# Mixer C's upward products as twelve pairs by Strassen's algorithm; the last two blocks' downward products joined there and in the first feed-forward layer

## What is computed

```
h = rmsnorm(x);  y = concat(a_out, b_out) @ w_out           # stage 0, mixer A/B
h = rmsnorm(x);  z = h @ w_up; g, up = split(z)             # stage 1, feed-forward layer 1, D_FF = 2816
                 y = (silu(conv3(g)) * up) @ w_down
h = rmsnorm(x);  z = h @ w_in; bg, cg, hx = split(z)        # stage 2, mixer C, width 1024
                 y = (bg * conv3(cg * hx)) @ w_out
h = rmsnorm(x);  ...                                        # stage 3, feed-forward layer 2
y = rmsnorm(x, norm_final)
```

## Time and profile before

| | us |
|---|---|
| median of 3 runs | 2181.38 (2180.86 to 2185.6) |
| the profiled execution | 2185.06, its span 2183.2 |
| PE busy | 2130.8 (98% of the span) |
| DVE, ACT, POOL busy | 1444.9 (66%), 675.8 (31%), 884.2 (40%) |
| from the last pair of stage 1 to the first matmul of stage 3 | 423.00 |

### The profile page before, as it was taken

The page is one execution under the profiler, slowest core; times in us unless marked ns, Lnnn a source line. Parts: engine busy times, 40 slices in busy tenths (PEclk is TensorE's granted clock), DMA queues, the critical chain, the costliest instruction groups (busy, mean ns, idle before and its releaser), DMA issues. The chain is left out here.

```text
span 2183.2 us, 35348 instructions
## 1 busy us (share of the span) xinstructions
PE 2130.8 (98%) x15116; PEld 2118.0 (97%) x15116; DVE 1444.9 (66%) x1765; ACT 675.8 (31%) x1002; POOL 884.2 (40%) x540
## 2 busy tenths in 40 slices
PE   6999999999999999999999999999999999999996
PEld 6999999999999999999999999999999999999996
DVE  5899769766666666666653524497666666766666
ACT  4555245322223322222311011263222223322233
POOL 4766234444434443434412221344343444444345
PEclk9999999999999999999999999999999999999998
DMA  4111210111111111111111111101111111111112
GB/s 160 39 39 41 109 61 30 59 39 59 39 59 59 49 40 49 59 40 59 49 39 49 49 49 39 49 30 45 53 57 41 59 59 40 39 59 49 49 42 80
DMA packets 33996, 115.31 MB, mean 53 GB/s; under 512 B 3824, under 2 KB 7408, under 8 KB 33840
## 3 DMA queue, kind: packets, MB, share of 16 engines
q1 hardware_dynamic: 33840, 113.06, 15.0%
HBM read 108.42 MB, written 4.62 MB: 52 GB/s over the span
## 5 line engine op out<-in xcount | busy, mean ns | idle before, releaser
L606 PE MATMUL psum<-xs_hi,w_hi 128*128 128x264 f32 (+1 forms) x3728 | 1112.7, 298 | 32.7 <-DVE xs_lo L1609 17.2
L608 PE MATMUL psum<-xs_hi,w_lo 128*128 128x264 f32 (+1 forms) x3728 | 1110.3, 298 | 0.0
L607 PE MATMUL psum<-xs_lo,w_hi 128*128 128x264 f32 (+1 forms) x3728 | 1106.3, 297 | 0.0
L1044 POOL TENSOR_TENSOR w_lo<-raw,w_hi 128x512 fp32r<-128x512 f32 (+1 forms) x358 | 595.0, 1674 | 983.5 <-ACT w_hi L1221 624.2
L606 PEld LDWEIGHTS psum<-xs_hi,w_hi 128*128 128x128 f32 x3728 | 702.6, 188 | 39.1 <-issue 11.4
L608 PEld LDWEIGHTS psum<-xs_hi,w_lo 128*128 128x128 f32 x3728 | 703.3, 189 | 0.0
L607 PEld LDWEIGHTS psum<-xs_lo,w_hi 128*128 128x128 f32 x3728 | 702.6, 188 | 0.0
L606 PE MATMUL psum<-act_hi,w_hi 128*128 128x352 f32 x1152 | 373.3, 324 | 0.1
L608 PE MATMUL psum<-act_hi,w_lo 128*128 128x352 f32 x1152 | 373.1, 324 | 0.0
L607 PE MATMUL psum<-act_lo,w_hi 128*128 128x352 f32 x1152 | 370.5, 322 | 0.0
L1620 DVE TENSOR_TENSOR x<-psum,x 128x704 f32<-128x704 f32 x208 | 185.0, 889 | 163.0 <-PE psum L608 162.2
(11 more groups left out here) (233 smaller groups left out, 1757.3 us busy)
## 6 DMA issues: line engine op xcount, KB each, us to landing
raw<-slabs SPq DMA_DIRECT2D x188, 512.0 KB, 3.2
x<-x_t SPq DMA_DIRECT2D x16, 528.0 KB, 6.9
y_t<-x SPq DMA_DIRECT2D x6, 528.0 KB, 3.4
y_t<-x SPq DMA_DIRECT2D x3, 352.0 KB, 2.3
x<-mix SPq DMA_DIRECT2D x1, 512.0 KB, 3.3
x<-bs SPq DMA_DIRECT2D x1, 256.0 KB, 3.9
tail_hi<-consts SPq DMA_DIRECT2D x1, 132.0 KB, 11.2
const<-consts SPq DMA_DIRECT2D x1, 130.0 KB, 4.4
```

What stands on the lines that cost most here:

```text
L606: nc.tensor.matmul(out, w_hi[:, w], hi, start=start, stop=False, skip_group_check=reopen)
L607: nc.tensor.matmul(out, w_hi[:, w], lo, start=False, stop=False, skip_group_check=reopen)
L608: return nc.tensor.matmul(out, w_lo[:, w], hi, start=False, stop=stop, skip_group_check=reopen)
L1044: nc.gpsimd.tensor_tensor(w_lo[:, slab], src, w_hi[:, slab].bitcast(F32), ALU.subtract).then_inc(weights_ready, 1)
```

## The change

1. **Mixer C in pairs.** The 24 upward tiles become twelve pairs in the code of the feed-forward stages: for each of four blocks of two channel tiles, (Cg, hx) of the first, (Cg, hx) of the second, and (Bg of the first, Bg of the second). `_units` lists three pairs a block for stage 2, `down` for blocks 0 and 1, and a `join` at the end. All three pairs use one up buffer, `prod[0]`; PSUM sets alternate by `x_set`.
2. **Joins.** The last two blocks' downward products of stages 1 and 2 are one pass over four activation tiles (`join`), eight output tiles of 4 products x 3 chunks x 3 = 36 matmuls, so that the next stage's normalised input is made as each output tile ends (`last_down`). Stage 1 had two passes of two before.
3. **Start.** 44 transposes of the identity on PE ahead of the data; ACT makes all eight high parts before any square; DVE makes all the sums of squares; ACT copies the first tile out of PSUM unscaled; the statistics stand after five of eight input tiles of the second job and the spread after all of them.
4. **Mixer A/B.** One GpSimd tap of channel tile 2 moves from slot 8 to slot 9 of `A_PLAN`.
5. **End.** The last product's chunks are 400, 400 and 256 frames; DVE makes all outputs of the second and third chunk; the second chunk's spread stands after the last matmul.

The diff, cut to its core: `up_free` is ACT's, ahead of its copy of group 0's result into the up buffer, `c_gate` (Cg x hx), `finish` and the second `join` are DVE's (the tables for semaphore counts, renamings and the host's packing of weights are left out):

```diff
+WARM_UP = 44
-FINAL_ROWS = [[(CUTS[c] + 88 * t, 88) for t in range(4)] for c in range(3)]
+FINAL_CUTS = (0, 400, 800, COLS)
+FINAL_ROWS = [[(FINAL_CUTS[c] + rows * t, rows) for t in range(n)] for c, (n, rows) in enumerate([(4, 100), (4, 100),
+                                                                                                (2, P)])]
+def _units(p):
+    pairs, last = (3 if p == 2 else 2), BLOCKS[p] - 1
+    units = []
+    for b in range(last + 1):
+        units += [("pair", b, q) for q in range(pairs)]
+        if b and (b < last or p == 3):
+            units.append(("down", b - 1))
+    return units + [("down", last) if p == 3 else ("join", last)]
...
+            def first_jobs():
+                up_job(0, 0, 0, fresh=True)
+                ring1 = slab_ready(1)
+                up_part(1, ring1, range(0, 5))
+                pe.wait_ge(tile_evacuated, evacuated(0))
+                pe.wait_ge(squares_summed, DVE_SUMS)
+                rms_stats(0, psum[:, 0, CH + 2:CH + 2 + ROW_TILES])
+                up_part(1, ring1, range(5, KD)).then_inc(tile_done, 1)
+                rms_spread(0, psum[:, 3, CH + 30:CH + 30 + ROW_REST])
...
+            for _ in range(WARM_UP):
+                nc.tensor.transpose(psum[:, 7, 0:P], ident[:], ident[:])
...
+            def join(p, unit):
+                acts = ACT0[p] + 2 * unit[1] - 2
+                for m in range(KD):
+                    if m % 2 == 0:
+                        pe.wait_ge(weights_ready, step_of(p, unit, m // 2) + 1)
+                        slab = ring(p, unit, m // 2)
+                    if m == 0:
+                        for k in range(4):
+                            pe.wait_ge(act_ready, acts + k + 1)
+                            for i in range(2):
+                                if k == 0:
+                                    down_banks_free(p, unit, i)
+                                last = down_tile(i, slab, 4 * i + k, k, k, 4)
+                                if k == 3:
+                                    last.then_inc(tile_done, 1)
+                    elif m > 1:
+                        down_banks_free(p, unit, m)
+                        for k in range(4):
+                            last = down_tile(m % 2, slab, m % 2 * 4 + k, k, k, 4)
+                        last.then_inc(tile_done, 1)
...
-            for t in range(2, 12):
-                up_job(2, t, SLAB0[2] + t, t % 2)
+            stage(1)
+            stage(2)
+            stage(3)
...
             for c in range(3):
-                cols = chunk(c)
-                width = CUTS[c + 1] - CUTS[c]
+                cols = final_chunk(c)
+                width = FINAL_CUTS[c + 1] - FINAL_CUTS[c]
...
+            def up_free(p, unit):
+                _, b, q = unit
+                if unit == ("pair", 0, 1):
+                    act.wait_ge(t1_made, KP * p)
+                elif p != 2:
+                    act.wait_ge(act_ready, ACT0[p] + 2 * (b - 1) + q + 1)
+                elif q:
+                    act.wait_ge(c_gated, 2 * b + q)
+                else:
+                    act.wait_ge(product_done, ACT0[2] - ACT0[1] + 2 * b)
...
+            def c_gate(b, q):
+                g, up = conv_in, prod[0]
+                if (b, q) != (0, 0):
+                    dve.wait_ge(up_scaled, pair_number(2, b, q) - 1)
+                dve.tensor_tensor(g[:, 2:2 + SEQ], g[:, 2:2 + SEQ], up[:, 0:SEQ], ALU.mult)
+                sample = g[:, 2 + SAMPLE + GAP:2 + GAP_COLS]
+                dve.tensor_tensor(sample, sample, up[:, SAMPLE:COLS], ALU.mult).then_inc(c_gated, 1)
+                dve.wait_ge(c_gated, 2 * b + q + 1)
...
+            def finish(p, b, q):
+                gate_second_half(p, b, q)
+                if p != 2:
+                    convolve(p, b, q)
+                elif q < 2:
+                    c_gate(b, q)
+                    if (b, q) == (0, 1):
+                        dve.wait_ge(t2_ready, KP * p)
+                        dve.wait_ge(t4_ready, KP * p)
+                    convolve(p, b, q)
...
+            def join(p, unit):
+                b = unit[1]
+                q = 2 if p == 2 else 1
+                finish(p, b, q)
+                if p != 2:
+                    hidden_lo(p, b, 0)
+                finish_more(p, b, q, 1)
+                finish_more(p, b, q, 2)
+                if p == 2:
+                    hidden_lo(p, b, 0)
+                else:
+                    product(p, b, 1)
+                hidden_lo(p, b, 1)
...
-            chunk_y(1, 2, DVE_Y)
+            chunk_y(1, 2, KD)
             chunk_r(2)
-            chunk_y(2, 0, DVE_Y)
+            chunk_y(2, 0, KD)
```

More of the change, by code:

```diff
@@ new lines, in _units, with _places @@
+def _units(p):
[6 more added lines that the diff above has]
+    return units + [("down", last) if p == 3 else ("join", last)]
+UNITS = [None] + [_units(p) for p in (1, 2, 3)]
+JOIN = [None] + [UNITS[p][-1] for p in (1, 2)]
+def _places():
+    at = [AB_JOBS, AB_JOBS - 8, AB_SLABS, 2 * AB_SLABS, AB_SLABS]
+    table, starts = [None], [[0] * 5]
+    for p in (1, 2, 3):
+        starts.append(list(at))
+        table.append({})
+        for unit in UNITS[p]:
+            kind = "first" if unit == FIRST else unit[0]
+            if unit[0] != "pair":
+                at[3] += at[3] % 2
+            table[p][unit] = tuple(at)
+            at = [n + size for n, size in zip(at, SIZES[kind])]
+    starts.append(at)
+    return table, starts
@@ L1498, in pair @@
                 act.wait_ge(tile_done, group_done(p, b, q, 2))
-                nc.scalar.activation(two(half(prod[q], 0)), halves_of(x_bank), ACT.Copy).then_inc(part_copied, 1)
+                if p == 2 and before == FIRST:
+                    act.wait_ge(c_gated, 1)
+                nc.scalar.activation(two(half(up, 0)), halves_of(x_bank), ACT.Copy).then_inc(part_copied, 1)
                 entry_hi(p, b, q, 6)
+                if p == 2 and q == 0:
+                    hidden_hi(p, b - 1, 1)
                 act.wait_ge(tile_done, group_done(p, b, q, 3))
@@ L1504, in pair @@
                 else:
-                    act.wait_ge(tile_evacuated, pair_read(p, b, q, C11_READ))
-                nc.scalar.activation(two(half(prod[q], 1)), halves_of(Z_BANK), ACT.Copy).then_inc(part_copied, 1)
-                if q == 0 and b == 1:
+                    act.wait_ge(tile_evacuated, pair_read(p, unit, C11_READ))
+                nc.scalar.activation(two(half(up, 1)), halves_of(Z_BANK), ACT.Copy).then_inc(part_copied, 1)
+                if p != 2 and q == 0 and b == 1:
                     hidden_hi(p, 0, 1)
```

882 lines of the change are left out of this document (406 added, 476 removed).

## The result

The changed kernel takes 2153.1 us in the median of 4 runs (2151.88 to 2156.07), the kernel before 2182.9 on the same chip: ratio 0.9865, 95% interval 0.985 to 0.9879, so a gain of 29.8 us where 38.0 was forecast. The time is 1.1 us above the range. The profiled execution is the longest of the four, 2156.07, with a span of 2154.3. Two executions in all that follows, one of 7522 us and one of 2598 us of the kernel before, ran at a mean granted clock of 0.41 and 0.75 and are in no median.

A forecast was written before the change was run, and what follows sets the result against it. PE's matmuls plus a few waits were taken to bound the kernel. Gains of 27.2, 6.4, 1.6 and 2.8 sum to 38.0 us, from the median of 2181.38 to 2143.4; range 2138 to 2152 (8 in 10).

The forecast's parts named there:

- Inside Mixer C: Mixer C's pairs: ACT's copy must wait for Cg x hx, with 1.4 us left at worst; costed at nothing.
- Mixer C's pairs wait: Rival: single up buffer or residues make Mixer C's pairs wait, 1 us in each of 11; 2147 to 2156, chance 0.11.
- PE's idle time before groups 2 or 4: Sign of being wrong: PE idle there in Mixer C, with ACT's work as the releaser.
- The matmuls: Mixer C: 1728 wide matmuls at 160.0 ns become 2040 narrow ones at 121.7 ns, a gain of 28.2 us.
- the floor: Rival: Mixer C's narrow matmuls cost as much as wide ones, 160 ns; kernel 2221 us; slower given chance 0.02.
- the figures of the Trainium skill: Mixer C's matmuls: estimates of 99 ns at 264 columns and 110 at 352, a loss of 12 us; trace disagrees.
- Stage 1's join: 46.4 us plus a 2.3 us PE wait for the last activation tile; second weight slab costed at nothing, bound 0.5.
- The stage's start: Mixer C's start: 1.9 us for the last residual add and waits in first full pairs; bounds 0.9 and 6.5.
- The start: Program start: third job begins at 40.6 instead of 47.03, a gain of 6.4 us, bounds 4 and 7.5.
- Mixer A/B: PE's 1.89 us wait at 132.73 shrinks as a tap moves behind a copy: gain 1.6 us, bounds 0 and 1.9.
- The end: Program end: smaller last chunk and GpSimd out of the way, gain 2.8 us, bounds 0 and 5.
- The middle: From stage 1's last pair to stage 3: 423.00 us becomes 395.8, a gain of 27.2 us.

The follow-up runs named there:

- the first experiment: In Mixer C, VectorE's C22 addition, which PE's group 6 waits for, moved ahead of the second weight sum, against the changed kernel: 2149.74 us.
- the second: In Mixer C, the first weight slab of each downward pass and join rounded, split and waited for in halves, against the changed kernel: 2150.73 us.
- both edits: Changed kernel with C22 ahead of the second weight sum and the first slab of Mixer C's downward passes and join in halves: 2143.18 us.
- the changed kernel again: The changed kernel repeated unedited on the third chip, giving its second profile: 2152.69 us.

## Why the prediction was right and wrong

**The step that failed** is the one under "Inside Mixer C", "I cost it at nothing". It looked for one new wait, ACT's copy behind Cg x hx. That wait is there, 0.35 us in each of the three pairs for which the step left 1.4 us and feared 1. The slow steps were two early ones of its chain, not the product. VectorE and GpSimd at the start of the second pair of block 1 (T is 1149.63):

```profile
1147.63 2.37 DVE L2193 TENSOR_TENSOR work<-work,r_rows 128x1056 f32<-128x1056 f32 x1
1149.92 1.21 DVE L1678 TENSOR_TENSOR act_lo<-work,act_hi 128x1024 fp32r<-128x1024 f32 x1
1151.06 1.28 DVE L1678 TENSOR_TENSOR act_lo<-work,act_hi 128x32 fp32r<-128x32 f32 x1
...
1153.73 1.23 DVE L2080 TENSOR_TENSOR work<-work 128x1024 f32<-128x1024 f32 x1
```

```profile
1147.60 1.29 POOL L1063 TENSOR_TENSOR w_lo<-raw,w_hi 128x512 fp32r<-128x512 f32 x1 [1.64 <-ACT w_hi L1234]
1150.54 1.76 POOL L1063 TENSOR_TENSOR w_lo<-raw,w_hi 128x512 fp32r<-128x512 f32 x1 [1.65 <-ACT w_hi L1234]
```

The scaling took 2.37 us (1.26 elsewhere) and ended at T+0.4 where the step had T-0.8; the 32 last columns of the low part took 1.28 (0.18 elsewhere) and ended at T+2.7 for T+0.7. Both began while a weight split ran on GpSimd. The product ran with GpSimd idle, in 1.23 us, and ended at T+5.4 for T+3.8. ScalarE's copy ended at T+6.1 for T+4.4. So the chain was 1.7 us late, more than the 1.4 of room.

Two things were overlooked:
- The copy and C22 are steps of queues that also feed the weights of the next pair. A late C11 passes through ACT and GpSimd to a sum that stands ahead of C22 on VectorE: four waits, 4.9 us. That C22's place behind the sum makes them is shown by the first experiment, which moved one step past another and removed them; why C11 is late is read from the rows.
- Three pairs of seven entries leave the ring at an odd position, and the padding makes two of the three slabs wait for group 5 in place of group 4: 3.2 us. That the slab is held by its later position is shown by the second, which lets each half go by itself. The order of positions could be read in the code; I had counted seven splits a pair and no parity.

With 1.0 us for the waits ahead of group 2 that is 9.2 us, and 8.4 of it came back with both edits. The case that happened is the rival "Mixer C's pairs wait" (0.11; 2147 to 2156), whose price, 1 us in each pair, was near, though not the residues and copy that it named. Saying that PE's idle time before groups 2 or 4 would show me wrong was half right: it was 2, 6 and the slabs.

**The other terms.**
- The matmuls: 121.7 ns, as read from the earlier trace rows; the floor did not come in. Neither did the figures of the Trainium skill (TensorE: Matmul & The Clock Gate, section Back-to-back issue gap).
- Stage 1's join: 2.05 us idle, 2.2 by distance, for 2.3. Its second weight slab, costed at nothing, was 0.2 us late in the second profile of this kernel. Mixer C's join: 46.49 for 46.4. The stage's start: 1.0 for 1.9, near its lower bound.
- The start: the third job at 41.67 in the first profile, behind a low stretch of 1.20 us, and at 40.41 and 40.58 in two executions without one (the changed kernel again, and both edits), for 40.6. That GpSimd's sums cost 3 us of statistics is shown by the run that brings them back, that the transposes have no part worth counting by the run without. The rest of the gain, the quicker low parts, was not tested alone.
- Mixer A/B: 1.7 for 1.6. The end: 4.1 for 2.8.
- The middle: 16.8 us for 27.2 between the two profiles. Of the 10.4 that are missing, 9.2 are the waits in Mixer C and 1.5 the low stretch behind the join's wait; 0.9 comes back at the stage's start, and 0.6 is in no term. The 1.2 us of low stretch in the 423.00 before were in the forecast gain too: without low stretches the middle is 421.8 before and 405.3 in the second profile of the changed kernel, a gain of 16.5.

With 6.6 for the start (47.03 to 40.41) these terms make 29.2 of the 29.8 us measured. They come from different executions, some with low stretches and some without, so that they meet to 0.6 us is in part luck. So is it that the kernel with both edits, 2143.18, meets the forecast of 2143.4: its end gave 1.3 us more than forecast and its middle 1.0 less. Of the four terms three held within their bounds, and the middle was 10 us too large.

The range was too narrow for the reason that the rival's upper half was cut off: a cost put at nothing with a chain of seven steps and 1.4 us of room on an engine busy for 90% of the pair deserved more than 0.11.

## What to carry to other kernels

When an engine that is not the bound comes to 90% busy, list what is queued behind every wait that it makes, not only the new one: here a step whose inputs were ready stood for 3.4 us behind one that waited for another engine. When units of odd size share a ring with units of even size, write down the position of each large one and what it waits for. Where a chain has little room, look which of its steps begin while the other engine runs, for these were the ones that took longer. And before two single profiles are compared, take the low stretches out of both: here they made 5 us between two executions of one kernel.

## What the runs showed of the hardware

- **Low stretches come and go.** PE's matmuls stood at twice their distance for 0.9 to 5.6 us at a time. Of ten profiled executions without transposes there, six had such a stretch behind the 2.05 us wait in stage 1's join (1.5 to 1.6 us lost each) and four did not, with the same wait; the two with them had none. That would fit an answer to idle time, but two are too few to tell from four of ten. Others came behind short waits (0.54 us ahead of the one at 34.34). Whether one can be kept away stays open; in the medians the transposes gave nothing.

A window of the first profile after, at the start of stage 3, where the last wait was one of 0.91 us some 9 us before, and the granted clock was 0.62:

```profile
1429.00:1433.50 4.50, 4.50 (x26) 4.47 (x26) 4.46 (x7) 2.93 (x7) 1.43 (x1) 0.62 0.64 233
```

- **A VectorE operation on SBUF took longer if it began while GpSimd ran.** A sum of 512 columns took 0.68 or 1.77 us, a tap 1.32 or 2.24, a product of 1024 columns 1.23 or 2.21, a scaling of 1056 columns 1.26 or 2.37, a low part of 32 columns 0.18 or 1.28: 0.9 to 1.1 us more, whatever the width. For the weight sums of the first profile (L1916, L1917, L1921) it goes by who began first: all 37 that began while a GpSimd operation ran took 1.73 to 1.78 us, and the 33 that a GpSimd operation joined later took 0.67 to 0.69, as did the 89 that met none. Some longer operations began in the last 0.4 us of one of GpSimd's and kept their length. Additions that read PSUM (L2155, L2162, L2167, 528 columns) always took 0.69 to 0.71.
- **GpSimd is slower there too.** Its split of 512 columns took 1.29 us where it began first (1147.60 in the timeline above) and 1.76 where VectorE's low part had begun 0.6 us before it (1150.54), and its sum of 1056 columns took 3.0 us beside VectorE's sums.
